# A two-block transformer on one core: the last block's sigmoid from an exponential, the table load in front of it, and the first half's root ahead of the second gate

## The reference

```
ple_gate = sigmoid(rmsnorm_2(h, ple_norm_w) @ w_ple_gate)
h = h + ple_gate * (p @ w_ple_proj)
return rmsnorm_2(h, final_norm_w)     # x * rsqrt(mean(x*x) + 1e-6) * w
```

## Time and profile before

| | us |
|---|---|
| median of 3 runs | 1219.64 |
| lowest and highest run | 1218.92, 1220.97 |
| the profiled execution's own time | 1219.4 |
| its span, first to last instruction | 1217.6 |
| start of the last matmuls (L1320) in it | 1208.1 |
| start and end of the eight last multiplications | 1208.95, 1213.86 |

### The profile page before, as it was taken

One profiled execution on the slowest core, in us unless ns is written; L12 is line 12 of the kernel. 1 busy time (PEld: TensorE's weight loads), 2 busy tenths in 40 slices (PEclk: granted clock), 3 DMA queues, 4 the chain that ended last, 5 costly groups with the idle time before them and its releaser, 6 DMA issues.

```text
span 1217.6 us, 15969 instructions
## 1 busy us (share of the span) xinstructions
PE 1189.4 (98%) x6548; PEld 959.4 (79%) x6548; DVE 711.5 (58%) x1094; ACT 497.0 (41%) x795; POOL 70.5 (6%) x62
## 2 busy tenths in 40 slices
PE   8999999999999999999999889999999999999996
PEld 5888778777776887877777789878888888888885
DVE  6776455567558765538886873454444444333356
ACT  5416524534534455115438444343232332322244
POOL 0190000003000100000000200000000000000000
PEclk9999999999999999999999999999999999999998
DMA  9762122122212433221222000122233222433322
GB/s 370 296 220 88 52 87 69 67 77 70 68 54 66 138 104 119 92 87 53 70 70 69 19 19 20 69 88 102 89 102 104 87 104 85 156 99 97 100 87 70
DMA packets 35593, 118.22 MB, mean 97 GB/s; under 512 B 3936, under 2 KB 6112, under 8 KB 35520
## 3 DMA queue, kind: packets, MB, share of 16 engines
q1 hardware_dynamic: 33024, 111.03, 27.0%
q0 software_dynamic: 1392, 4.72, 1.3%
q10 hardware_dynamic: 1104, 1.45, 0.3%
HBM read 112.99 MB, written 4.19 MB: 96 GB/s over the span
## 4 chain that ended last, share of the span: by engine, by line
PE 86%; DVE 5%; ACT 5%; issue 1%; DVEq 0%; ACTq 0%
PE pb L651 84%; PE pb L906 1%; PE pb L737 1%; ACT mP L1532 1%; DVE mnm L2061 1%; DVE xT L1817 1%; ACT whi L1341 1%; DVE wlo L1817 1%; ACT Y L1341 1%; DVE mP L2051 1%; PE pb L1068 0%; DVE tmpf L1817 0%; ACT xT L1553 0%; ACT fv L1341 0%; DVE hlo L1820 0%
## 5 line engine op out<-in xcount | busy, mean ns | idle before, releaser
L651 PE MATMUL pb<-hhi,wlo 128*128 128x512 f32 (+2 forms) x1048 | 407.4, 389 | 2.6 <-DVE wlo L1817 2.6
L651 PE MATMUL pb<-hlo,whi 128*128 128x512 f32 (+2 forms) x1048 | 405.4, 394 | 1.7 <-DVE hlo L1820 0.7
L651 PE MATMUL pb<-hhi,whi 128*128 128x512 f32 (+2 forms) x1048 | 406.8, 388 | 0.0
L1817 DVE TENSOR_TENSOR wlo<-raw,whi 128x1024 fp32r<-128x1024 f32 (+2 forms) x177 | 216.4, 1226 | 111.1 <-ACT whi L1341 110.2
L651 PEld LDWEIGHTS pb<-hlo,whi 128*128 128x128 f32 (+1 forms) x1048 | 197.0, 188 | 46.7 <-issue 3.5
L651 PEld LDWEIGHTS pb<-hhi,wlo 128*128 128x128 f32 (+1 forms) x1048 | 196.5, 188 | 44.2 <-DVE wlo L1817 3.5
L651 PEld LDWEIGHTS pb<-hhi,whi 128*128 128x128 f32 (+1 forms) x1048 | 196.3, 187 | 41.0
L1341 ACT ACTIVATE whi<-raw 128x1024 fp32r<-128x1024 f32 (+2 forms) x177 | 180.3, 1035 | 76.5 <-PE pb L651 55.7
L651 PE MATMUL pb<-alo,whi 128*128 128x512 f32 x176 | 68.5, 389 | 0.0
L651 PE MATMUL pb<-ahi,wlo 128*128 128x512 f32 x176 | 68.5, 389 | 0.0
L651 PE MATMUL pb<-ahi,whi 128*128 128x512 f32 x176 | 68.5, 389 | 0.0
(11 more groups left out here) (368 smaller groups left out, 1603.7 us busy)
## 6 DMA issues: line engine op xcount, KB each, us to landing
raw<-w_all SPq DMA_DIRECT2D x165, 512.0 KB, 3.5
adab<-ada_d SPq DMA_DIRECT2D x12, 512.0 KB, 12.7
gbt<-ada_d SPq DMA_DIRECT2D x12, 512.0 KB, 8.5
raw<-w_all SPq DMA_DIRECT2D x10, 384.0 KB, 3.0
xT<-xn_d SPq DMA_DIRECT2D x4, 512.0 KB, 12.7
ple_scratch<-zs SPq DMA_DIRECT2D x8, 256.0 KB, 5.7
xT<-x_d POOLq DMA_DIRECT2D x8, 256.0 KB, 3.2
out_d<-xT SPq DMA_DIRECT2D x6, 256.0 KB, 2.6
```

What stands on the lines that cost most here:

```text
L651: return e.matmul(out, lhs, rhs, start=start, stop=stop, skip_group_check=True)
L1817: return e.tensor_tensor(out, a, b, op)
```

## The change

For block 7 ACT takes exp(-x) instead of tanh(x/2), and DVE makes the rest of the sigmoid: add 1 and multiply by 0.5, take the reciprocal (2 sigmoid(x)), multiply by `plr`. That is a `tensor_scalar`, a `reciprocal` and a `tensor_tensor` for each half in place of one `scalar_tensor_tensor`, each waiting for the one ahead. The other blocks keep Tanh.

The `EXPLN` table is loaded behind the Tanh of block 6. ACT's order becomes: Tanh of block 6, load, Exp of (7, 0), `gated` of block 6, `gated` of (7, 0), root of half 0, Exp of (7, 1), root of half 1. The wait for a free `sq` buffer in `gated` of half (7, 0) is now for block 5's sum, no longer for block 6's. DVE's order becomes: `gate_in` of (7, 0), `gate_out` of (7, 0), `squared` of block 6, `gate_in` of (7, 1) and so on. TensorE's, SP's and POOL's programs are the same.

```diff
@@ -1773,14 +1773,17 @@
             def gate(k):
                 m, c = k[1], half(k)
                 A.wait_ge(*SCALED(k))
-                e.activation(tmpf[:, m % 2, c], tmpf[:, m % 2, c], ACT.Tanh, scale=0.5).then_inc(PGT.sem, 1)
+                if m < 7:
+                    e.activation(tmpf[:, m % 2, c], tmpf[:, m % 2, c], ACT.Tanh, scale=0.5).then_inc(PGT.sem, 1)
+                else:
+                    e.activation(tmpf[:, m % 2, c], tmpf[:, m % 2, c], ACT.Exp, scale=-1.0).then_inc(PGT.sem, 1)
 
             def gated(k):
 
                 m, c = k[1], half(k)
                 A.wait_ge(*TXR(k))
                 if m > 2:
-                    A.wait_ge(*SS(("p", min(m - 2, 5) + (m == 7))))
+                    A.wait_ge(*SS(("p", m - 2)))
                 e.activation(sq[:, 1 - m % 2, c] if m else ssq[:, :], xT[:, m, c], ACT.Square).then_inc(SQ.sem, 1)
                 copy(xT[:, m, c], xT[:, m, c], scale=vc(V_LN + m)).then_inc(XSC.sem, 1)
 
@@ -1795,12 +1798,14 @@
             for m in range(7):
                 gate(("p", m))
                 conv("pg", m)
-                gated(("p", m))
+                if m < 6:
+                    gated(("p", m))
+            e.preload_act_table_set(EXPLN)
             gate(("p", 7, 0))
+            gated(("p", 6))
             gated(("p", 7, 0))
+            last_root(0)
             gate(("p", 7, 1))
-            e.preload_act_table_set(EXPLN)
-            last_root(0)
             last_root(1)
             A.wait_ge(*SQD())
             copy(xT[:, 7, 256:512], xT[:, 7, 256:512], scale=vc(V_LN + 7)).then_inc(XSC.sem, 1)
@@ -2452,7 +2457,14 @@
                 m, c = k[1], (slice(256 * k[2], 256 * k[2] + 256) if len(k) > 2 else slice(0, S))
                 s_ = tmpf[:, m % 2, c]
                 V.wait_ge(*PGT(k))
-                stt(s_, s_, 1.0, plr[:, m % 4, c], ALU.add, ALU.mult).then_inc(PGM.sem, 1)
+                if m < 7:
+                    stt(s_, s_, 1.0, plr[:, m % 4, c], ALU.add, ALU.mult).then_inc(PGM.sem, 1)
+                else:
+                    e.tensor_scalar(s_, s_, 1.0, 0.5, ALU.add, ALU.mult).then_inc(DVS.sem, 1)
+                    V.wait_ge(*DVS.tick())
+                    e.reciprocal(s_, s_).then_inc(DVS.sem, 1)
+                    V.wait_ge(*DVS.tick())
+                    tt(s_, s_, plr[:, m % 4, c], ALU.mult).then_inc(PGM.sem, 1)
                 V.wait_ge(*PGM(k))
                 tt(xT[:, m, c], xT[:, m, c], s_, ALU.add).then_inc(TXR.sem, 1)
 
@@ -2467,6 +2479,7 @@
                     V.wait_ge(*PLIN[7]())
                     V.wait_ge(*TXR(("p", 5)))
                     gate_in(("p", 7, 0))
+                    gate_out(("p", 7, 0))
                 squared("p", m)
             def last_norm(i, q):
                 V.wait_ge(*RSQ((f"fin{i}", "exp")))
@@ -2474,7 +2487,6 @@
                 r = sq[:, 1, 256 * i:256 * i + 256].rearrange("p (a b) -> p a b", a=1).to_broadcast([128, 2, 256])
                 tt(done_at(i, q), done_at(i, q), r, ALU.mult).then_inc(FIN.sem, 1)
 
-            gate_out(("p", 7, 0))
             gate_in(("p", 7, 1))
             gate_out(("p", 7, 1))
             V.wait_ge(*TXR(("p", 7, 1)))
```

## The result

| | before | changed |
|---|---|---|
| median of 16 runs, us | 1219.09 | 1222.14 |
| lowest to highest | 1216.39 to 1220.97 | 1219.34 to 1223.17 |
| profiled execution: its own time, its span | 1219.4, 1217.6 | 1219.34, 1217.5 |

A forecast was written before the change was run, and what follows sets the result against it. TensorE, busy 98% of the span, bounds the kernel, so only work behind its last matmuls counts. Half 0's +2.08 and half 1's +1.51 give +3.6 us on 1219.64: 1223.2 us, range 1220.5 to 1224.8.

The forecast's parts named there:

- The sum: Whole tail: half 0's +2.08 and half 1's +1.51 make the kernel +3.6 us slower.
- narrower one: Range of the main forecast, for a reciprocal of 1.35 to 2.5 us: 1222.1 to 1224.7 us, chance 0.64.
- The reciprocal's price: DVE, 128x256, once in each half: 1.95 us taken, from 7 ns per column and a fixed 150 ns.
- cheap reciprocal: Rival: DVE's reciprocal streams like other operations, 0.43 us, so +0.6 us in all; chance 0.31 for everything below 1.35.
- Half 0: TensorE waits for block 6's sum, queued on DVE behind half 0's `gate_out`; k = 7 starts +2.08 us later.
- Half 1: From half 1's `gate_in` to the last multiplications on DVE: 4.65 us where before 3.14, +1.51 us.
- The 0.15 us for the Exp queued behind the first root: ACT, half 1: the Exp starts at 1208.50 where its data would have allowed 1208.35.
- The load: ACT, table load moved behind block 6's Tanh: costs nothing, with 0.66 us of cover before half 0's Exp.
- rival of a longer load: ACT held beyond the load's 1.28 us, delaying the first Exp; at 2.56, +0.6 us on top; chance 0.02.
- The second root: ACT, half 1: ends at 1214.32, the fifth last multiplication wants it at 1214.94; covered by 0.6 us.
- the slow clock: TensorE at the 1.2 GHz level during k = 7 matmuls after longer stops: 0 to 1.1 us more, taken as 0.
- Order only pays: Faster rival: block 6's sum and reciprocal cost nothing, DVE's idle 0.89 us is saved: -0.4 us at most; chance 0.03.

The follow-up runs named there:

- y2: Changed kernel, but half 0 keeps Tanh, load behind it; ACT makes half 1's sigmoid; DVE fills waits with half 0's last multiplications: 0.9992 of before.
- x1: Changed kernel with the reciprocal left out in both halves, so block 7's gate is wrong: 0.9993 of before, tail 15.46 us.
- y5: As y2, plus 18 unused matmuls of 256 columns on TensorE behind k = 7: 0.9983 of before, tail 14.45 us.
- y1: Changed kernel with block 6's square and sum put first, and ACT making block 7's whole sigmoid (Exp, Ln, Exp), no reciprocal: 1.0005 of before.
- x2: Changed kernel with the reciprocal left out in half 0 alone: 1.0010 of before, tail 17.29 us.

## Why the prediction was right

**The sum.** I gave +3.6 us and the tails differ by 3.21, the medians by 3.05. The sign, the two places and most of the size came out. The time, 1223.2 forecast and 1222.14 measured, is off by 1.1 us: half of that is the sum, the other half the time to which it was added, since the median of before is 1219.09 in 16 runs and was 1219.64 in the three that I had. 1222.14 lies inside the range; that it also lies in the forecast's narrower one (1222.1 to 1224.7) hangs on 0.04 us and is luck. The upper end of that one was added wrongly: a reciprocal of 2.5 us gives 3.6 + 2 x 0.55 = +4.7, so 1224.3 us.

**The reciprocal's price** was the term mis-sized: 1.95 us taken, 1.75 measured. From the 178 ns for 4 columns to this, each column costs (1750 - 178)/252 = 6.2 ns, where I had 7. As it enters twice, this is the 0.4 us between 3.6 and 3.2. That the value I took came so near is in part luck: 28 ns at four columns were multiplied by 64, so 3 ns in the fixed part are the whole error. The cheap reciprocal (0.43 us) is refuted. The 8-column row was the better guide to the fixed part; the 4-column `tensor_scalar` would have given 1.0 us. The Trainium skill ("VectorE: DVE Perf Modes", section "First, the fixed hardware budget") says that the reciprocal is a divide with a repeat count of 8. My estimate from it, 8.3 ns per column, is too dear: the trace shows six times 1.04 ns. It pointed the right way, though, to a dear reciprocal.

**The `tensor_scalar`:** 0.29 us for 0.30.

**Half 0:** +2.08 taken, +2.05 measured, but not quite for my reasons. With a reciprocal of 1.75 my steps give +1.88. The 0.17 more lies in TensorE: from L1318 behind the stop to `gate_in` (7, 1) it took 1.52 us, where I had 1.34. I had put one pair of matmuls at 0.35 and the next at 0.25; they started 0.54 and 0.24 us ahead of what followed. Why the first pair behind this stop takes longer than L1320's behind its stop before (0.35) stays open.

**Half 1:** +1.51 taken, +1.14 measured. The reciprocal explains 0.2 of that. The 0.15 us for the Exp queued behind the first root were not paid: it started 0.48 us behind `gate_in`, as half 0's did (0.46). The first root's Ln had followed L1320 after 0.63 us, not 0.74, since those matmuls took 0.59 with no stop of their own, not 0.70. This error (-0.15) and the one in half 0 (+0.17) cancel, and that is luck too.

**The load** costs nothing at its new place: 0.68 us of cover were left, 0.66 expected. The rival of a longer load falls: in y2 the load ends at 1202.60 and the square behind it starts at 1202.62. The Trainium skill ("ScalarE: Activation LUTs", section "What ACT_TABLE_LOAD costs") has 1.38 us of drain beside the load; none of these traces shows it.

**The second root** was covered, but barely. Its Exp ended at 1211.15 and the fifth multiplication wanted it at 1208.83 + 4 x 0.60 = 1211.23: 0.1 us of my 0.6 was left. Here the prediction had missed something: it asked whether the slow clock would reach the matmuls of k = 7, but not whether it would reach the last sum. The last sum took 1.22 us at the lower clock, as the windows of the changed kernel show (columns as in the earlier trace rows):

```profile
1207.50:1208.50 1.00, 0.00 (x0) 0.00 (x0) 0.90 (x4) 0.00 (x0) 0.00 (x0) 1.00 0.00 0
...
1209.50:1210.50 1.00, 0.69 (x2) 0.00 (x0) 1.00 (x3) 0.27 (x1) 0.00 (x0) 0.50 0.02 7
```

**Order only pays**, the faster rival, was priced at -0.4 us at most, all of it in half 1; x1 measured -0.36 in the tail, as -0.64 in half 1 and +0.27 in half 0. So that the totals agree is in part luck: half 1 gained more than the rival had, and half 0, priced at nothing, lost.

## What to carry to other kernels

Price a removal by the wait that ends last with it gone: the 1.28 us load could give 0.89 us at most, and the whole idea gave 0.4 with the reciprocal left out. Before an operation goes onto a path that is crossed twice, price it at its real width: 178 ns at 4 columns left everything from 0.43 to 2.5 us open at 256. The neighbours by which I split off the fixed part did not agree (1.0 or 1.95 us), and nothing in the trace said which to trust. An early result pays only if somebody uses it early: the first root was ready 3.7 us before DVE's first multiplication, and only moving those multiplications (y2, y5) turned that into time.

## What the runs showed of the hardware that was not expected

A RECIPROCAL on 128x256 in float32 took 1.75 us on DVE, against 0.42 for a tensor_tensor of that size. Ln of (1 + x) and an Exp on ACT took 1.0 us for what `tensor_scalar` and reciprocal did in 2.1.

The granted clock does not follow from the length of one stop alone: in x1 the last sum ran at the lower level (1.22 us) behind a stop of 2.24 us, in y1 at the full one (0.70) behind a stop of 2.90. The changed kernel and x2 are the clearest pair: stops of 4.02 and 4.03 us in front of the last sum, which then took 1.22 us in one and 0.70 in the other. What decides it, these runs don't show. With eighteen unused matmuls, y5's profile had 1.00 up to the last sum. Where the slow sum was covered (changed, x1) it cost nothing; where it was the wait that ended last (y2) it cost 0.5 us.
